# Front of a hybrid layer: ada product by column tiles on TensorE, its loads by row blocks, x turned and projected in two halves

## Chip, core and metric

The kernel runs on one core of a Trainium2 chip. The metric is the device time of one execution in microseconds (us). TensorE is called PE in the profile (its weight loads PEld), VectorE DVE, ScalarE ACT, GpSimd POOL; SyncE (SP) only issues loads and stores. Everything is float32 unless told otherwise.

## What is computed

One layer on 1024 tokens of width 1024: modulated norm, a projection into four parts, a gated recurrence beside a spatial gating unit, an output projection, then a mixture of 32 experts with 4 per token. The change touches the first lines:

```python
c_act = jax.nn.silu(c)
mod = c_act @ ada_w[l] + ada_b[l]                    # [1, 1024] @ [1024, 6144]
sh1, sc1, g1, sh2, sc2, g2 = jnp.split(mod[:, None, :], 6, axis=-1)
z = rmsnorm(h, norm1_g[l]) * (1.0 + sc1) + sh1       # h = x, [1024, 1024]
proj = z @ w_in[l]                                   # [1024, 1024] @ [1024, 2048]
xa, ya, u, v = jnp.split(proj, [D_LRU, 2 * D_LRU, 2 * D_LRU + D_SGU], axis=-1)
```

`sh1` and `sc1` are the first 2048 of the 6144 ada columns; they alone are needed for `z`.

## The kernel before, in words

Five programs, one per engine, run beside one another and are ordered by semaphores. Engines other than SP and POOL work through their programs strictly in the order written.

**Order of loads.** `DENSE` (L55) is the list of 2 MB weight loads, in order: ada 0 to 3, win 0, ada 4, ada 5, win 1, and so on; "ada j" is columns 512 j to 512 j + 511 of `ada_w`, "win j" the same of `w_in`. They rotate through four slots of `big` (`ring`). SP (from L389) first loads 11 small parameter tensors, then runs through `DENSE`: loads 0 to 3 at once; ahead of load 4 (win 0) the eight x tiles of 128 tokens, 512 KB each (L398 to L400); from load 4 on each load waits until its slot is free: `gemv_made` counts finished ada products, `filled` counts PSUM banks that TensorE has filled. A load is laid out (k p) n -> p k n, so each of its rows in memory is 512 columns, 2 KB. POOL (L514) waits for the third `gemv_made` and then issues 13 small transfers (gating weights, gate matrices, biases, two blocks of zeros), 2.75 MB with many rows under 512 B.

**Order of banks.** `bank_jobs` (L69) is the list of everything that passes through the eight PSUM banks, in TensorE's order, with the engine that drains each; a job takes the bank of the job eight places ahead of it once that is drained. `open_bank`, `take` and `drained_before` turn the list into waits.

**Ada product (VectorE).** `mod_products(j)` (L1260) multiplies the eight row blocks of ada j with the eight columns of silu(c), one instruction of 128x512 each, adding up in `gacc[:, j % 2]`: one at L1267, seven at L1269. TensorE's `mod_cols(j)` (L861) sums over the partitions, four matmuls against a column of ones (L867), two instructions each; `mod_add(j)` (L1274) adds the bias. j = 0 to 3 come first; then `scale1` = norm1_g (1 + sc1) (L1290, L1291), which raises `affine_made`.

**x.** ScalarE squares each x tile as it lands (L658, scratch in the memory of `zT`, k = 0), takes the root (L659), for all eight tiles; then it waits for `affine_made` and drains the even k of `zT` (L666), first for tokens 0 to 511 (th = 0), then for the others. VectorE scales the eight tiles by their 1/rms (L1304, L1305) and drains the odd k (`modulate`, L1298). TensorE turns x: for each th and k four transposes of 128x128 into one bank (L898); th = 0 waits for four scaled tiles, th = 1 for eight. When both halves of `zT` are drained and win 0 is there, it projects `xa`: four m by two th, eight matmuls of 128x512 each, two instructions per matmul (`project`, L881).

**Behind it.** VectorE copies each bank of `xa` to `xaT` (L1354), runs `conv(0)` (L1329, L1331) and ada products 4 and 5 in between, then builds the rows of g1 (L1366, L1372). TensorE does `mod_cols(4)`, `mod_cols(5)`, the g1 rows (L875), the turning of the gating weights (L915), and then `ya` with `win 1`. Then follow gates, recurrence, `u`, `v`, output projection, router, and from about 520 us on the expert loop (L1118, L1144: matmuls in column tiles of 32).

Of the kernel before, what the change touches and what calls it, by code (L numbers as in the profile page):

```python
# [20 lines left out]
P = 128  # L21
# [47 lines left out]
def bank_jobs():  # L69

    jobs = [("cols", 0, "dve")]
    jobs += [("mod", j, "dve") for j in range(4)]
    jobs += [("zT", (k, th), "dve" if k % 2 else "act") for th in range(2) for k in range(KT)]
    jobs += [("xa", (m, th), "dve") for m in range(CT) for th in range(2)]
    jobs += [("mod", j, "dve") for j in (4, 5)]
# [57 lines left out]
def build(nc, ins, out):  # L133
# [8 lines left out]
    with ExitStack() as ctx:  # L142
        def sb(name, shape, dt=F32):
            return ctx.enter_context(nc.sbuf_tensor(name, shape, dt))
# [10 lines left out]
        def ring(key):  # L155
            return big[:, DENSE_AT[key] % DENSE_SLOTS, :].rearrange("p (k n) -> p k n", k=8)

        lru_t = big[:, 4, :].rearrange("p (i n) -> p i n", i=4)
        s5 = big[:, 5, :]
# [56 lines left out]
        cols = sb("cols", [P, NROWS])  # L216
        cact = sb("cact", [P, KT])
        mod = sb("mod", [P, 48])
# [171 lines left out]
        def _(sp_):  # L390
# [6 lines left out]
            for n, (kind, j) in enumerate(DENSE):  # L397
                if n == DENSE_SLOTS:  # L398
                    for t in range(TT):
                        sp_.dma_start(x_rows[:, t, :], x[t * P:(t + 1) * P, :]).then_inc(x_in[t], SEMW)  # L400
                if n >= DENSE_SLOTS:
                    old, i = DENSE[n - DENSE_SLOTS]
                    if old == "ada":
                        sp_.wait_ge(gemv_made, i + 1)
                    else:
                        last = ("v", TT - 1) if i == 3 else (("xa", "ya", "u")[i], (CT - 1, 1))
                        sp_.wait_ge(filled, JOB[last] + 1)
                w = {"ada": ada_w, "win": w_in, "wout": w_out}[kind]
                sp_.dma_start(ring((kind, j)), w[:, j * 512:(j + 1) * 512].rearrange("(k p) n -> p k n", p=P)
                              ).then_inc(dense_in[n % DENSE_SLOTS], SEMW)  # L410
# [63 lines left out]
        def _(pool):  # L474
            chain = [0]

            def link(ins_):

                chain[0] += 1
                ins_.then_inc(pool_chain, 1)  # L480
                pool.wait_ge(pool_chain, chain[0])

            link(pool.memset(ident[:, :], 0.0))
            link(pool.affine_select(out=ident[:, :], in_=ident[:, :], compare_op=ALU.not_equal, fill=1.0, base=0,
# [152 lines left out]
        def _(act):  # L637
# [15 lines left out]
            act.wait_ge(dve_drained, 1)  # L653
            act.activation(cact[:, :], cols[:, ROW["c"]:ROW["c"] + 8], ACT.Silu).then_inc(cact_made, 1)

# [194 lines left out]
        def _(pe):  # L850
# [38 lines left out]
            pe.transpose(b[:, 0:NROWS], prow[0:NROWS, :], ident[0:NROWS, 0:NROWS]).then_inc(filled, 1)  # L889
            for j in range(4):  # L890
                mod_cols(j)

            for th in range(2):
                pe.wait_ge(x_scaled, 4 * th + 4)
                for k in range(KT):
# [3 lines left out]
                    last.then_inc(filled, 1)  # L899
            dense_ready(("win", 0))  # L900
            for who, drained in (("act", act_drained), ("dve", dve_drained)):
                pe.wait_ge(drained, drained_before(JOB[("zT", (KT - 1, 1))], who))
            for m in range(CT):
                for th in range(2):
                    project("xa", ("win", 0), m, th)
# [328 lines left out]
        def _(dve):  # L1234
# [24 lines left out]
            def mod_products(j):  # L1259

                n = DENSE_AT[("ada", j)]
                dve.wait_ge(dense_in[n % DENSE_SLOTS], SEMW * (n // DENSE_SLOTS + 1))
                if j >= 2:

                    dve.wait_ge(filled, JOB[("mod", j - 2)] + 1)
# [9 lines left out]
            def mod_add(j):  # L1275
                b = take("mod", j)
                dve.tensor_tensor(mod[:, 4 * j:4 * j + 4], b[:, 0:4], col("ada_b", 4 * j, 4), ALU.add
                                  ).then_inc(dve_drained, 1)

            dve.wait_ge(cact_made, 1)  # L1280
            mod_products(0)
            mod_products(1)
            mod_add(0)
            mod_products(2)
            mod_add(1)
            mod_products(3)
            mod_add(2)
            mod_add(3)
            dve.wait_ge(dve_drained, drained_by(JOB[("mod", 3)])[1])
            link(dve.tensor_scalar(scale1[:, :], mod[:, SC1:SC1 + 8], 1.0, None, ALU.add))  # L1290
# [10 lines left out]

            for t in range(TT):
                dve.wait_ge(sqrt_made, t + 1)
                link(dve.reciprocal(rstd[:, t:t + 1], srt[:, t:t + 1]))  # L1304
                dve.tensor_scalar(x_rows[:, t, :], x_rows[:, t, :], rstd[:, t:t + 1], None, ALU.mult).then_inc(x_scaled, 1)  # L1305
            for th in range(2):
                modulate("zT", th, lambda k: zT[:, k, th * 512:(th + 1) * 512], scale1, SH1)

# [42 lines left out]
            for m in range(CT):  # L1351
                for th in range(2):
                    b = take("xa", (m, th))
                    dve.tensor_copy(xaT[:, m, th * 512:(th + 1) * 512], b).then_inc(dve_drained, 1)  # L1354
                if m == 0:
                    dve.wait_ge(dve_drained, drained_by(JOB[("xa", (0, 1))])[1])
                    conv(0)
                if m < 2:
                    mod_products(4 + m)
# [348 lines left out]
```

## Time and profile before

| what | value |
|---|---|
| median of 3 runs | 2366.47 us (2357.96, 2366.47, 2366.7) |
| profiled execution, its own time | 2362.14 us |
| its span, first to last instruction | 2360.4 us |
| instructions | 53160 |
| TensorE busy | 2133.1 us, 90% |
| VectorE, ScalarE, GpSimd busy | 767.7, 387.2, 436.2 us |
| mean granted TensorE clock | 0.961 |
| DMA | 525.82 MB, mean 223 GB/s |
| gate/up and down matmuls of the expert loop (L1118, L1144) | 1021.9 and 529.3 us busy |

"Idle before, releaser" in a row tells how long the engine stood still ahead of it and what ended that. Rows of SPq and POOLq are issues of transfers, not their duration. A granted clock of 1.00 is 2.4 GHz, 0.50 is 1.2 GHz.

### The profile page before, as it was taken

To read this page: it belongs to the slowest core of one execution; us is meant where nothing else is said; L and a number is where in the kernel's file an instruction comes from. 1 tells how busy PE (TensorE), PEld (TensorE's weight loads), DVE (VectorE), ACT (ScalarE), POOL (GpSimd) and SP (SyncE) were. 2 spreads that over 40 slices of the span, in tenths; PEclk is the share of its full clock that TensorE was granted. 3 is DMA by queue.
4 is the path that set the end of the run, shared out by engine and by line. 5 is a ranking of instruction groups with operands and counts; after the bars stand their busy time and mean duration, and the time that the engine had idled before them with its cause. 6 is when DMAs were issued, how large, how long until landed. Compare 5 with 4: busy or idle time off the path is not lost.

```text
span 2360.4 us, 53160 instructions
## 1 busy us (share of the span) xinstructions
PE 2133.1 (90%) x21037; PEld 921.1 (39%) x21038; DVE 767.7 (33%) x2033; ACT 387.2 (16%) x866; POOL 436.2 (18%) x420
## 2 busy tenths in 40 slices
PE   3998989949999999999898879889999888989995
PEld 3443444423443434334333224334443333443342
DVE  6437744242323222222223223223222232222223
ACT  3035122121111111011111101111111111010112
POOL 2000022021222122222212112212221221221221
PEclk9999999969999999999999899989999999999997
DMA  9312215141653529365499999599988659944345
GB/s 335 114 62 107 107 42 228 69 150 35 222 171 125 215 56 366 96 238 191 149 390 347 403 390 380 206 402 383 398 320 316 223 186 401 371 150 140 95 163 171
DMA packets 142462, 525.82 MB, mean 223 GB/s; under 512 B 14672, under 2 KB 45376, under 8 KB 109664
## 3 DMA queue, kind: packets, MB, share of 16 engines
q1 hardware_dynamic: 111728, 470.39, 51.6%
q0 software_dynamic: 30704, 55.06, 10.0%
q8 instruction: 15, 0.25, 0.0%
q14 instruction: 15, 0.12, 0.0%
HBM read 493.02 MB, written 32.37 MB: 223 GB/s over the span
## 4 chain that ended last, share of the span: by engine, by line
PE 69%; DMA 9%; issue 8%; DVE 7%; ACT 2%; POOL 2%; SPq 2%; DVEq 1%; POOLq 0%; ACTq 0%
PE psum L1118 32%; PE psum L1144 19%; PE psum L1014 4%; PE psum L881 4%; DMA r<-hs_rows,idx_next 3%; DMA big<-in_exp_w_gu_dram 3%; PE psum L976 2%; DMA big<-in_exp_w_down_dram 2%; PE psum L1085 1%; PE psum L1130 1%; PE psum L1072 1%; DMA big<-in_w_in_dram 1%; POOL r L595 1%; DVEq L341 1%; PE psum L923 1%
## 5 line engine op out<-in xcount | busy, mean ns | idle before, releaser
L1118 PE MATMUL psum<-big,r 128*32 128x512 f32 x9152 | 1021.9, 600 | 32.2 <-DMA big<-in_exp_w_gu_dram 31.5
L1118 PEld LDWEIGHTS psum<-big,r 128*32 128x32 f32 x9152 | 285.6, 110 | 684.7 <-issue 624.0
L1144 PE MATMUL psum<-big,r 128*32 128x256 f32 x9152 | 529.3, 385 | 18.2 <-issue 14.0
L1144 PEld LDWEIGHTS psum<-big,r 128*32 128x32 f32 x9152 | 293.6, 111 | 228.8 <-issue 53.6
L588 POOL DMA_INDIRECT acc_rows<-r,sidx_cur x143 | 225.3, 1576 | 497.1 <-DVE r L1640 467.2
L788 ACT ACTIVATE r<-r 128x256 f32<-128x256 f32 x143 | 59.3, 414 | 1266.3 <-DVE r L1627 1266.3
L595 POOL TENSOR_TENSOR r<-r 128x256 f32<-128x256 f32 x143 | 104.3, 730 | 831.6 <-ACT r L788 831.6
L1621 DVE TENSOR_TENSOR r<-psum,r 128x256 f32<-128x256 f32 x143 | 60.7, 425 | 519.1 <-PE psum L1118 519.1
L1637 DVE TENSOR_TENSOR r<-psum,r 128x256 f32<-128x256 f32 x143 | 60.7, 424 | 432.0 <-PE psum L1144 432.0
L881 PE MATMUL psum<-r,big 128*128 128x512 f32 x384 | 167.9, 598 | 1.4 <-DMA big<-in_w_in_dram 1.4
L781 ACT ACTIVATE r<-psum,mod,scale 128x128 f32<-128x128 f32 x384 | 141.9, 460 | 28.0 <-PE psum L1085 28.0
L1085 PE MATMUL psum<-ident,r 128*128 128x128 f32 x384 | 68.4, 307 | 54.9 <-DMA r<-hs_rows,idx_next 54.9
L1632 DVE TENSOR_TENSOR r<-r 128x256 f32<-128x256 f32 x143 | 60.8, 425 | 168.7 <-POOL r L595 168.7
L1014 PE MATMUL psum<-big,r 128*128 128x512 f32 x256 | 111.1, 594 | 0.6 <-DMA big<-in_w_out_dram 0.4
L881 PEld LDWEIGHTS psum<-r,big 128*128 128x128 f32 x384 | 73.2, 192 | 92.9 <-issue 91.3
L793 ACT ACTIVATE r<-psum 128x256 f32<-128x256 f32 x143 | 55.1, 386 | 296.3 <-PE psum L1130 296.3
L1085 PEld LDWEIGHTS psum<-ident,r 128*128 128x128 f32 x384 | 48.9, 156 | 94.9 <-DMA r<-hs_rows,idx_next 62.2
L1014 PEld LDWEIGHTS psum<-big,r 128*128 128x128 f32 x256 | 48.3, 190 | 62.6 <-issue 61.3
L577 POOL DMA_INDIRECT r<-hs_rows,idx_next x48 | 48.1, 1003 | 128.4 <-DVE idx_next L1588 125.8
L1640 DVE SCALAR_TENSOR_TENSOR r<-r,g1row 128x256 f32<-128x256 f32 x143 | 69.4, 485 | 5.1
L1130 PE MATMUL psum<-ident,r 128*128 128x128 f32 x286 | 62.0, 300 | 6.4 <-DVE r L1632 6.4
L1269 DVE SCALAR_TENSOR_TENSOR gacc<-big,cact,gacc 128x512 f32<-128x512 f32 x84 | 63.1, 752 | 3.0
(233 smaller groups left out, 1118.8 us busy)
## 6 DMA issues: line engine op xcount, KB each, us to landing
big<-in_exp_w_gu_dram SPq DMA_DIRECT2D x256, 1024.0 KB, 7.7
big<-in_exp_w_down_dram SPq DMA_DIRECT2D x128, 1024.0 KB, 16.2
big<-in_ada_w_dram SPq DMA_DIRECT2D x12, 2048.0 KB, 12.9
r<-in_x_dram SPq DMA_DIRECT2D x16, 512.0 KB, 12.6
big<-in_w_in_dram SPq DMA_DIRECT2D x4, 2048.0 KB, 19.1
r<-in_exp_b_gu_dram SPq DMA_DIRECT2D x128, 64.0 KB
big<-in_w_out_dram SPq DMA_DIRECT2D x2, 2048.0 KB, 13.3
hs_rows<-r POOLq DMA_DIRECT2D x8, 512.0 KB, 3.2
```

Of the source, the lines that this page charges most:

```text
L588: pool.indirect_dma_start(acc_quarters, bass.IndirectOffsetOnAxis(ap=sidx_cur[:, u:u + 1], axis=0), y_sb[:, u, :], None, bounds_check=4 * ...
L595: pool.tensor_tensor(gsig_sb[:, u % 2, :], gate_sb[:, u % 2, :], sig_sb[:, u % 2, :], ALU.mult).then_inc(gsig_made, 1)
L781: ins_ = act.activation(izT[:, k, :], psum[:, 6 + half, i * P:(i + 1) * P], ACT.Identity, bias=mod[:, SH2 + k:SH2 + k + 1], scale=scale2[: ...
L881: last = pe.matmul(b, w[:, k, m * P:(m + 1) * P], zT[:, k, th * 512:(th + 1) * 512], start=(k == 0), stop=(k == KT - 1))
L1014: last = pe.matmul(b, src[:, ct % CT, t * P:(t + 1) * P], ring(("wout", dh))[:, ct, :], start=(ct == 0), stop=(ct == 2 * CT - 1))
L1085: last = pe.transpose(psum[:, 6 + half, i * P:(i + 1) * P], zg[:, k * P:(k + 1) * P], ident[:, :])
L1118: last = pe.matmul(psum[32 * j:32 * j + 32, u, :].rearrange("p (a n) -> p a n", a=2), izT[:, k, u * UNIT:(u + 1) * UNIT], rhs[:, :, 256 * ...
L1130: last = pe.transpose(psum[:, u, h * P:(h + 1) * P], act_sb[:, u % 2, h * P:(h + 1) * P], ident[:, :])
L1144: ins_ = pe.matmul(psum[32 * i:32 * i + 32, 4 + u % 2, 0:256], actT[:, u, h, 32 * j:32 * j + 32], down_slab(f)[:, 256 * i:256 * i + 256], ...
L1269: ins_ = dve.scalar_tensor_tensor(out=a, in0=w[:, k, :], scalar=cact[:, k:k + 1], in1=a, op0=ALU.mult, op1=ALU.add)
L1632: dve.tensor_tensor(act_sb[:, u % 2, :], lin_u, gsig_sb[:, u % 2, :], ALU.mult).then_inc(act_made, 1)
L1640: dve.scalar_tensor_tensor(out=y_sb[:, u, :], in0=y_sb[:, u, :], scalar=sgate_cur[:, u:u + 1], in1=g2_rows, op0=ALU.mult, op1=ALU.mult).th ...
```

## The change

The first 2048 columns of the ada product go to TensorE. Loads 0 to 3 of `DENSE` become row blocks: load j brings rows 256 j to 256 j + 255, all 2048 columns (rows of 8 KB). silu(c) is written into column 0 of eight 32-column stationary tiles `cact_cols`, whose other columns are zero. For each k, four matmuls write four column tiles (32 partitions each) of one bank, one for each 512 columns; the sum over all k ends there as four rows, at partitions 0, 32, 64 and 96. VectorE copies the bank to `gacc`, and four matmuls against every 32nd column of `ident` put the 2048 sums back on the partitions (job "mods"). x tiles 0 to 3 are issued ahead of win 0, tiles 4 to 7 behind it. TensorE turns and projects tokens 0 to 511, then the others. VectorE's program follows that order. ScalarE's program changes in one line, the destination of silu(c).

```diff
@@ -68,10 +68,10 @@
 
 def bank_jobs():
 
-    jobs = [("cols", 0, "dve")]
-    jobs += [("mod", j, "dve") for j in range(4)]
-    jobs += [("zT", (k, th), "dve" if k % 2 else "act") for th in range(2) for k in range(KT)]
-    jobs += [("xa", (m, th), "dve") for m in range(CT) for th in range(2)]
+    jobs = [("cols", 0, "dve"), ("ada", 0, "dve"), ("mods", 0, "dve")]
+    for th in range(2):
+        jobs += [("zT", (k, th), "dve" if k % 2 else "act") for k in range(KT)]
+        jobs += [("xa", (m, th), "dve") for m in range(CT)]
     jobs += [("mod", j, "dve") for j in (4, 5)]
     jobs += [("g1row", q, "dve") for q in range(2)]
     jobs += [("wm", q, "dve") for q in range(2)]
@@ -155,6 +155,9 @@
         def ring(key):
             return big[:, DENSE_AT[key] % DENSE_SLOTS, :].rearrange("p (k n) -> p k n", k=8)
 
+        def ada_pair(j):
+            return big[:, j, :].rearrange("p (k n) -> p k n", k=2)
         lru_t = big[:, 4, :].rearrange("p (i n) -> p i n", i=4)
         s5 = big[:, 5, :]
         ln_g = s5[:, 0:512]
@@ -214,7 +217,8 @@
         before = lru_t[:, 0, 0:P]
         prow = r2[:, 0:P]
         cols = sb("cols", [P, NROWS])
-        cact = sb("cact", [P, KT])
+        cact_cols = sb("cact_cols", [P, KT, UNIT])
+        cact = cact_cols[:, :, 0]
         mod = sb("mod", [P, 48])
         scale1 = sb("scale1", [P, KT])
         scale2 = sb("scale2", [P, KT])
@@ -395,8 +399,8 @@
                 sp_.dma_start(prow[ROW[name]:ROW[name] + rows, :], src.rearrange(pat, p=P)).then_inc(param_in, SEMW)
 
             for n, (kind, j) in enumerate(DENSE):
-                if n == DENSE_SLOTS:
-                    for t in range(TT):
+                if n in (DENSE_SLOTS, DENSE_SLOTS + 1):
+                    for t in range(4 * (n - DENSE_SLOTS), 4 * (n - DENSE_SLOTS) + 4):
                         sp_.dma_start(x_rows[:, t, :], x[t * P:(t + 1) * P, :]).then_inc(x_in[t], SEMW)
                 if n >= DENSE_SLOTS:
                     old, i = DENSE[n - DENSE_SLOTS]
@@ -405,6 +409,11 @@
                     else:
                         last = ("v", TT - 1) if i == 3 else (("xa", "ya", "u")[i], (CT - 1, 1))
                         sp_.wait_ge(filled, JOB[last] + 1)
+                if n < DENSE_SLOTS:
+                    sp_.dma_start(ada_pair(j), ada_w[2 * P * j:2 * P * (j + 1), 0:2048].rearrange("(k p) n -> p k n", p=P)
+                                  ).then_inc(dense_in[n], SEMW)
+                    continue
                 w = {"ada": ada_w, "win": w_in, "wout": w_out}[kind]
                 sp_.dma_start(ring((kind, j)), w[:, j * 512:(j + 1) * 512].rearrange("(k p) n -> p k n", p=P)
                               ).then_inc(dense_in[n % DENSE_SLOTS], SEMW)
@@ -480,6 +489,7 @@
                 ins_.then_inc(pool_chain, 1)
                 pool.wait_ge(pool_chain, chain[0])
 
+            link(pool.memset(cact_cols[:, :, :], 0.0))
             link(pool.memset(ident[:, :], 0.0))
             link(pool.affine_select(out=ident[:, :], in_=ident[:, :], compare_op=ALU.not_equal, fill=1.0, base=0,
                                     pattern=[[-1, P]], channel_multiplier=1))
@@ -651,7 +661,7 @@
 
             act.wait_ge(const_made, 1)
             act.wait_ge(dve_drained, 1)
-            act.activation(cact[:, :], cols[:, ROW["c"]:ROW["c"] + 8], ACT.Silu).then_inc(cact_made, 1)
+            act.activation(cact, cols[:, ROW["c"]:ROW["c"] + 8], ACT.Silu).then_inc(cact_made, 1)
 
             for t in range(TT):
                 act.wait_ge(x_in[t], SEMW)
@@ -887,8 +897,24 @@
             pe.wait_ge(const_made, 1)
             b = open_bank("cols", 0)
             pe.transpose(b[:, 0:NROWS], prow[0:NROWS, :], ident[0:NROWS, 0:NROWS]).then_inc(filled, 1)
-            for j in range(4):
-                mod_cols(j)
+            b = open_bank("ada", 0)
+            pe.wait_ge(cact_made, 1)
+            for n in range(4):
+                dense_ready(("ada", n))
+                for kk in range(2):
+                    k = 2 * n + kk
+                    for i in range(4):
+                        last = pe.matmul(b[32 * i:32 * i + 32, :], cact_cols[:, k, :], ada_pair(n)[:, kk, 512 * i:512 * i + 512],
+                                         start=(k == 0), stop=(k == KT - 1), skip_group_check=True)
+                last.then_inc(gemv_made if n < 3 else filled, 1)
+            b = open_bank("mods", 0)
+            wait_drained(pe, JOB[("ada", 0)])
+            for i in range(4):
+                last = pe.matmul(b[:, 4 * i:4 * i + 4], gacc[:, 0, i * P:(i + 1) * P], ident[:, 0:P:UNIT],
+                                 start=(i == 0), stop=True, skip_group_check=True)
+                if i == 0:
+                    last.then_inc(gemv_made, 1)
+            last.then_inc(filled, 1)
 
             for th in range(2):
                 pe.wait_ge(x_scaled, 4 * th + 4)
@@ -897,11 +923,10 @@
                     for i in range(4):
                         last = pe.transpose(b[:, i * P:(i + 1) * P], x_rows[:, 4 * th + i, k * P:(k + 1) * P], ident[:, :])
                     last.then_inc(filled, 1)
-            dense_ready(("win", 0))
-            for who, drained in (("act", act_drained), ("dve", dve_drained)):
-                pe.wait_ge(drained, drained_before(JOB[("zT", (KT - 1, 1))], who))
-            for m in range(CT):
-                for th in range(2):
+                dense_ready(("win", 0))
+                for who, drained in (("act", act_drained), ("dve", dve_drained)):
+                    pe.wait_ge(drained, drained_before(JOB[("zT", (KT - 1, th))], who))
+                for m in range(CT):
                     project("xa", ("win", 0), m, th)
             for j in (4, 5):
                 mod_cols(j)
@@ -1260,7 +1285,7 @@
 
                 n = DENSE_AT[("ada", j)]
                 dve.wait_ge(dense_in[n % DENSE_SLOTS], SEMW * (n // DENSE_SLOTS + 1))
-                if j >= 2:
+                if j >= 6:
 
                     dve.wait_ge(filled, JOB[("mod", j - 2)] + 1)
                 w, a = ring(("ada", j)), gacc[:, j % 2, :]
@@ -1277,16 +1302,20 @@
                 dve.tensor_tensor(mod[:, 4 * j:4 * j + 4], b[:, 0:4], col("ada_b", 4 * j, 4), ALU.add
                                   ).then_inc(dve_drained, 1)
 
+            def scale_x(t):
+                dve.wait_ge(sqrt_made, t + 1)
+                link(dve.reciprocal(rstd[:, t:t + 1], srt[:, t:t + 1]))
+                dve.tensor_scalar(x_rows[:, t, :], x_rows[:, t, :], rstd[:, t:t + 1], None, ALU.mult).then_inc(x_scaled, 1)
             dve.wait_ge(cact_made, 1)
-            mod_products(0)
-            mod_products(1)
-            mod_add(0)
-            mod_products(2)
-            mod_add(1)
-            mod_products(3)
-            mod_add(2)
-            mod_add(3)
-            dve.wait_ge(dve_drained, drained_by(JOB[("mod", 3)])[1])
+            b = take("ada", 0)
+            dve.tensor_copy(gacc[:, 0, :], b).then_inc(dve_drained, 1)
+            scale_x(0)
+            b = take("mods", 0)
+            dve.tensor_tensor(mod[:, 0:16].rearrange("p (i b) -> p b i", b=4), b[:, 0:16].rearrange("p (b i) -> p b i", b=4),
+                              col("ada_b", 0, 16).rearrange("p (i b) -> p b i", b=4), ALU.add).then_inc(dve_drained, 1)
+            dve.wait_ge(dve_drained, drained_by(JOB[("mods", 0)])[1])
             link(dve.tensor_scalar(scale1[:, :], mod[:, SC1:SC1 + 8], 1.0, None, ALU.add))
             dve.tensor_tensor(scale1[:, :], scale1[:, :], col("norm1_g", 0, 8), ALU.mult).then_inc(affine_made, 1)
             dve.wait_ge(affine_made, 1)
@@ -1299,12 +1328,15 @@
                                       ).then_inc(dve_drained, 1)
 
 
-            for t in range(TT):
-                dve.wait_ge(sqrt_made, t + 1)
-                link(dve.reciprocal(rstd[:, t:t + 1], srt[:, t:t + 1]))
-                dve.tensor_scalar(x_rows[:, t, :], x_rows[:, t, :], rstd[:, t:t + 1], None, ALU.mult).then_inc(x_scaled, 1)
-            for th in range(2):
-                modulate("zT", th, lambda k: zT[:, k, th * 512:(th + 1) * 512], scale1, SH1)
+            for t in range(1, 4):
+                scale_x(t)
+            modulate("zT", 0, lambda k: zT[:, k, 0:512], scale1, SH1)
+            for t in range(4, TT):
+                scale_x(t)
+            for m in range(CT):
+                b = take("xa", (m, 0))
+                dve.tensor_copy(xaT[:, m, 0:512], b).then_inc(dve_drained, 1)
+            modulate("zT", 1, lambda k: zT[:, k, 512:1024], scale1, SH1)
 
             dve.wait_ge(sp_exp, 2)
             link(dve.tensor_scalar(sp[:, 3, :], sp[:, 2, :], 2.0, None, ALU.add))
@@ -1349,9 +1381,8 @@
                 dve.wait_ge(lru_made, ct + 1)
 
             for m in range(CT):
-                for th in range(2):
-                    b = take("xa", (m, th))
-                    dve.tensor_copy(xaT[:, m, th * 512:(th + 1) * 512], b).then_inc(dve_drained, 1)
+                b = take("xa", (m, 1))
+                dve.tensor_copy(xaT[:, m, 512:1024], b).then_inc(dve_drained, 1)
                 if m == 0:
                     dve.wait_ge(dve_drained, drained_by(JOB[("xa", (0, 1))])[1])
                     conv(0)
```

## Rows read from the trace of the kernel before

**Rows 1.** the page: span, and busy time with share of each engine

```profile
span 2360.4 us, 53160 instructions
...
PE 2133.1 (90%) x21037; PEld 921.1 (39%) x21038; DVE 767.7 (33%) x2033; ACT 387.2 (16%) x866; POOL 436.2 (18%) x420
```

**Rows 2.** chain of waits, 20 to 125 us (start, us, what)

```profile
25.50 28.87 DMA big<-in_w_in_dram
...
54.41 55.20 PE psum L881 x128
...
117.44 7.73 PE psum L881 x18
```

**Rows 3.** timeline of SP's queue, 0 to 60 us (start, us, what)

```profile
4.84 9.95 SPq L409 DMA_DIRECT2D big<-in_ada_w_dram  x4
14.83 10.63 SPq L400 DMA_DIRECT2D r<-in_x_dram  x8
25.50 0.98 SPq L409 DMA_DIRECT2D big<-in_w_in_dram  x1
```

**Rows 4.** windows: busy us by engine, clock, DMA share, GB/s

```profile
20.00:28.00 8.00, 2.64 (x12) 2.47 (x12) 7.64 (x13) 0.00 (x0) 0.00 (x0) 1.00 1.05 387
28.00:36.00 8.00, 1.86 (x8) 1.78 (x8) 7.64 (x13) 5.59 (x11) 4.93 (x8) 1.00 1.04 409
36.00:44.00 8.00, 2.67 (x12) 2.59 (x13) 5.83 (x16) 5.25 (x12) 4.05 (x6) 1.00 1.03 281
1240.00:1250.00 10.00, 10.00 (x92) 3.23 (x88) 3.91 (x13) 3.30 (x9) 2.19 (x3) 1.00 1.01 421
```

**Rows 5.** timeline of ScalarE, 28 to 60 us

```profile
30.31 1.06 ACT L658 ACTIVATE r<-r 128x1024 f32<-128x1024 f32 x1 [20.93 <-DMA r<-in_x_dram]
...
44.47 1.06 ACT L658 ACTIVATE r<-r 128x1024 f32<-128x1024 f32 x1 [2.06 <-DMA r<-in_x_dram]
...
45.85 1.43 ACT L666 ACTIVATE r<-psum,mod,scale 128x512 f32<-128x512 f32 x2
```

**Rows 6.** timeline of POOL, 0 to 60 us

```profile
31.07 1.15 POOL L515 DMA_DIRECT2D r<-in_sgu_w_dram  x1 [24.14 <-DVE gacc L1269]
```

**Rows 7.** timeline of all engines: turning and draining x

```profile
43.20 9.81 PE L898 MATMUL psum<-ident,r 128*128 128x128 f32 x64 [4.56 <-DVE r L1305]
...
48.62 5.24 DVE L1298 TENSOR_SCALAR r<-psum,scale,mod 128x512 f32<-128x512 f32 x6 [0.25 <-PE psum L898]
```

**Rows 8.** timelines: column tiles, single 32-column matmuls, mod reduction

```profile
546.56 3.64 PE L1118 MATMUL psum<-big,r 128*32 128x512 f32 x32
...
478.78 7.03 PE L1001 MATMUL psum<-r,big 128*32 128x512 f32 x16 [0.20 <-ACT r L764]
...
24.82 1.87 PE L867 MATMUL psum<-ones,gacc 128*128 128x1 f32 x8 [4.04 <-DVE gacc L1269]
```

**Rows 9.** windows: transposes (L898) alone twice, then all of TensorE

```profile
43.00:48.00 5.00, 4.80 (x23) 4.81 (x24) 1.00 1.03 340
49.00:53.00 4.00, 4.00 (x37) 3.77 (x35) 1.00 1.04 408
...
114.00:116.00 2.00, 2.00 (x4) 0.81 (x4) 0.69 (x1) 0.00 (x0) 0.00 (x0) 0.50 1.05 407
```

**Rows 10.** expert loop: windows with the clock, first and second gate stage

```profile
523.60:526.00 2.40, 2.33 (x12) 0.68 (x16) 0.92 (x6) 0.00 (x0) 0.39 (x1) 0.50 0.00 0
...
523.67 22.15 PE L1118 MATMUL psum<-big,r 128*32 128x512 f32 x192 [0.49 <-issue]
...
571.44 20.74 PE psum L1118 x192
```

**Rows 11.** timeline of VectorE, 60 to 118 us

```profile
68.45 0.69 DVE L1354 COPY r<-psum 128x512 f32<-128x512 f32 x1 [6.17 <-PE psum L881]
...
73.87 0.48 DVE L1267 TENSOR_SCALAR gacc<-big,cact 128x512 f32<-128x512 f32 x1
74.38 5.48 DVE L1269 SCALAR_TENSOR_TENSOR gacc<-big,cact,gacc 128x512 f32<-128x512 f32 x7
```

## Prediction

> **What bounds the kernel now.** I read the page first: TensorE is busy for 90% of the span [rows 1], and the costly groups lie in the expert loop, which the change does not touch. So the change can only move the moment at which the rest starts. I then read the chain of waits for the first 125 us [rows 2]. SP issues loads; the load of `win 0` ends that stretch, 28.87 us after its issue; TensorE runs the `xa` projection from 54.41 to 109.61; small steps follow, and `ya` starts at 117.44. Two paths meet at 54.4: the bytes of `win 0`, and x scaled, turned and modulated. The second ends with VectorE's last drain at 48.62 + 5.24 = 53.86 [rows 7], only 0.5 us earlier. After `xa`, every load is released by work on TensorE or VectorE (`filled`, `gemv_made`), so nothing behind `xa` is tied to the start of the program: **the change is worth what it moves the end of `xa`**, with no cushion and no discount.
>
> The DMA queue is the second thing to see. SP issues ada 0 to 3, eight x tiles and `win 0` [rows 3], and its queue lands them in that order. The engines are full all the time, at 387 GB/s on the 2 KB rows of ada, 409 with the 4 KB rows of x, 281 while POOL's small transfers mix in [rows 4]. ScalarE gets the first x tile at 30.31 and the last at 44.47, and only after squaring the last one does it start on the `zT` drains, at 45.85 [rows 5].
>
> **Bytes.** Moved are four ada blocks (8.39 MB), four x tiles (2.10), `win 0` (2.10), then the other four x tiles (2.10). Up to the last x tile these are the same 14.7 MB that ended with `win 0` before, and POOL's transfers lie in front of it both times: released by the third `gemv_made`, they went out from 31.07 on [rows 6]; now the third block releases them at about 25, and they still end before 53. The issue of `win 0` now waits for block 0's product (about 15 us), with 10 MB already queued: nothing. Ada rows become 8 KB wide. The nearest row for that width is a stretch of expert weights at 421 GB/s; 8.39 MB take 21.7 us at 387 and 19.9 at 421, between 0 and 1.8 saved, I take 1.5. So the last x tile lands at 54.4 - 1.5 = **52.9** (before: 44.5), and `win 0` some 5 us ahead of it. The Trainium skill (DMA: Bandwidth & Descriptors, section Bandwidth) says that loads from HBM are bound near 358 GB/s per core; by that wider rows would save nothing and everything would come 1.5 us later. The trace does not agree: it is at 387 to 421.
>
> **The ada product.** Removed: four passes of eight VectorE instructions, about 6 us each (0.48 + 5.48 us, [rows 11]), and their 16 small matmuls. Each of the four small reductions on TensorE takes 1.87 us [rows 8]. Added: 32 matmuls of 32 columns by 512, two instructions each, in four column tiles. The expert loop shows such groups: 32 instructions in 3.64 us, against 16 in 7.03 for single 32-column matmuls one after another [rows 8]. So a block of 16 instructions costs 1.8 us, twice that at the lower clock; blocks land 5 us apart, and the last, at about 27, is worked off by 31. The copy (0.7), four matmuls against ident (at most 1.9), the addition (0.2) and scale1 (0.6) give scale1 at about 35. Nothing waits for it before 52.9: free, with 18 us of cover. POOL's added memset (0.3 us) hides behind the first ada landing.
>
> **x, first half.** Tile 3 lands in the middle of POOL's transfers, near 39; squared and scaled by 42; 32 transposes. These ran 23 in 5 us early and 37 in 4 us later [rows 9], so the first half takes up to 6.9 us and is turned by 49. VectorE drains the odd k. **ScalarE does not drain the even k**: its program is not in the diff. It squares all eight tiles, then drains. It sits on tile 4 to 7 with the zT drains queued behind, TensorE waits for those drains ahead of `xa`, and the first half's early start is lost. From tile 7: square to first drain 45.85 - 44.47 = 1.38 us, four drains about 2.75 (two take 1.43, [rows 5]), 0.1 to wake: `xa` starts at **57.1** instead of 54.41, **+2.7**.
>
> **Clock.** TensorE then has been idle since about 49. After such a pause, at the start of the expert loop, the granted clock is 0.50 (the 1.2 GHz level) up to 526, and 192 instructions take 22.15 us against 20.74 [rows 10]. Bounds 0 and 1.6; I take **+1.4**. Before, the pause was 1.4 us.
>
> **The turn between the halves.** Before, all 64 transposes stood ahead of `xa`. Now 32 stand between its halves, exposed: 32 at 37 in 4 us are 3.5 us, the last VectorE drain 0.85 behind (53.86 against 53.01), 0.1 to wake. That is **+4.4**. Bounds: 3.0, if drains follow closer, and 7.5 at the earlier rate of the transposes. The halves themselves are the same 128 instructions, 55.2 us.
>
> **VectorE in the second half.** conv(0) and two ada products must now fit into 27.6 us instead of 55. Copy, convolution and product 4 took 68.45 to 79.86 [rows 11], 11.4 us; a copy and product 5 add 6.7, and a copy 0.7. From the first full bank (6.9) that is 25.7: 1.9 us of cover, gone if anything there gets longer, and then TensorE's `mod 5` step would wait. I cost it at nothing. The scale_x of tiles 4 to 7 and the `zT` drains of half 1 are on VectorE ahead of this and inside the terms above.
>
> **Sum.** 2.7 + 1.4 + 4.4 = +8.5 us: `xa` ends at 118.1 instead of 109.6. The profiled execution took 2362.14 us (span 2360.4), so it would be 2370.6. It lies 4.3 below the median of the three runs, 2366.47; against that median: **2375.0**. That is 0.36% slower, and about 0.5% (11.8 us) is what a measurement can tell from no change: the runs alone lie 8.7 us apart. So I call it "same", on the slow side.
>
> **Rivals.**
> *A, the halves do overlap with the loads as drawn (faster).* If tiles 4 to 7 were there before ScalarE needs them, `xa` would start when half 0 is turned, at 49 (`win 0` lands at 47 to 48): 49.2 + 27.6 + 4.4 + 27.6 = 108.8, 0.8 us less than before, 2365.7. For it: the ada path is free early. Against: 17.4 MB would have to land by 45, at 458 GB/s over 38 us, and no row shows more than 421. Even then the gain stays inside 0.5%. Chance 5%.
> *B, the clock falls in the turn (slower).* If transposes do not keep TensorE at the 2.4 GHz level, the second half's 32 take the early rate, 0.22 us each (7.0 instead of 3.5), and its projection starts at 1.2 GHz (+1.4): +13.4 in all, 2379.9. It decides when 4.4 us without a plain matmul let the clock fall. For it: between 109.6 and 113.7 small matmuls did not hold it (0.50 from 114 to 116, [rows 9]), and the rate of the early transposes was the lower one. Against: in that same run of transposes the rate rose to 37 in 4 us with nothing but transposes running [rows 9]. The Trainium skill (TensorE: Matmul & The Clock Gate, Part 4) says that transposes do not count as busy for the clock in the same way, which would give this case; the row speaks against it. Chance 14%.
> *C, the column tiles do not overlap.* Then a block costs 6.9 us at full clock and 13.8 at half; the product would end between 41 and 68, and the halves are turned only behind it: in the second case `xa` starts near 79 instead of 57.1, 2397. [rows 8] speak against it. Chance 2%.
> *Forecast*: 79%.
>
> **How the numbers follow.** The forecast's own terms run from 2.4 + 0 + 3.0 = +5 (ada rows at the full 421, no cold start, drains close behind) to 4.2 + 1.6 + 4.4 = +10 (no gain from wider rows; a longer turn is case B), and the scatter of medians adds some 3 us to either side. The range, **2365 to 2382**, takes in A and B and leaves out C and the far scatter. Slower by over 0.5%: half or more of B, all of C, an eighth of the forecast, 0.19. Faster by over 0.5%: scatter alone, 0.03. Within: 0.78.
>
> **What would show it.** Right: ScalarE's square of the last x tile at about 53 and the first `zT` drain over 1 us later; TensorE idle from about 49 to 57 although `win 0` has landed; `xa` in two stretches of 27 to 29 us with 4.4 us between them; its end near 118; the rest shifted unchanged. Wrong: the last x tile before 48, ScalarE draining `zT` before it, a clock of 0.50 behind the turn (B), scale1 later than 50 (C), a wait of TensorE at `mod 5`, or `ya` starting less late than `xa` ends.

## The result, and the profile after

The changed kernel takes 2372.52 us (median of 10 runs, 2367.96 to 2381.77) against 2365.23 of the kernel before (10 runs); the ratio is 1.0041, with a 95% interval of 1.0025 to 1.0057. By the ratio that is +9.7 us, by the plain difference of the two medians +7.3; forecast were +8.5. The time lies inside the range of 2365 to 2382, and the change is inside 0.5%, on the slow side. The profiled execution took 2371.42 us, its span is 2369.7, 9.3 more than before.

ScalarE first. Timeline of the changed kernel from 28 us on; line numbers have moved (L668 squares x, L676 drains `zT`, L924 turns x, L891 projects, L907 is the ada product):

```profile
28.78 1.06 ACT L668 ACTIVATE r<-r 128x1024 f32<-128x1024 f32 x1 [19.02 <-DMA r<-in_x_dram]
...
34.57 1.06 ACT L668 ACTIVATE r<-r 128x1024 f32<-128x1024 f32 x1 [0.30 <-DMA r<-in_x_dram]
...
49.43 1.06 ACT L668 ACTIVATE r<-r 128x1024 f32<-128x1024 f32 x1 [13.38 <-DMA r<-in_x_dram]
...
53.54 1.04 ACT L668 ACTIVATE r<-r 128x1024 f32<-128x1024 f32 x1
...
54.91 2.77 ACT L676 ACTIVATE r<-psum,mod,scale 128x512 f32<-128x512 f32 x4
```

The first x tile is there at 28.78, where [rows 5] had 30.31: the 8 KB rows saved 1.5 us over the four ada blocks, as taken. Tile 3 is squared at 34.57. Then ScalarE stands still for 13.38 us until tile 4 lands at 49.43, squares four tiles without a pause, and drains the first even k of half 0 only at 54.91. TensorE meanwhile (timeline of PE):

```profile
27.51 1.93 PE L907 MATMUL psum<-big,cact_cols 128*32 128x512 f32 x16 [1.62 <-DMA big<-in_ada_w_dram]
...
37.08 5.10 PE L924 MATMUL psum<-ident,r 128*128 128x128 f32 x32 [5.70 <-DVE r L1309]
57.77 30.73 PE L891 MATMUL psum<-r,big 128*128 128x512 f32 x64 [15.59 <-ACT r L676]
88.34 3.66 PE L924 MATMUL psum<-ident,r 128*128 128x128 f32 x32
93.10 27.70 PE L891 MATMUL psum<-r,big 128*128 128x512 f32 x64 [1.11 <-DVE r L1327]
```

The last ada block takes 1.93 us, half 0 is turned by 42.2, and 15.59 us pass until ScalarE's drain lets the first half of `xa` start at 57.77. The profile puts the wait down to ScalarE (ACT), not to a load. The first half takes 30.73 us, the second 27.70; between them 32 transposes and 1.11 us of waiting for VectorE's drain. `xa` ends at 120.80; it was 109.61 [rows 2]. The chain of waits runs through the same points:

```profile
16.75 32.66 DMA r<-in_x_dram
...
57.77 30.73 PE psum L891 x64
88.50 3.51 PE psum L924 x32
92.03 0.82 DVE r L1327
```

And the granted clock in the first microseconds of `xa` (windows: PE, PEld, DVE, ACT, POOL busy, clock, DMA share, GB/s):

```profile
57.70:60.00 2.30, 2.23 (x3) 1.17 (x4) 0.00 (x0) 0.00 (x0) 0.00 (x0) 0.50 1.05 387
...
62.00:64.00 2.00, 2.00 (x4) 0.80 (x3) 0.00 (x0) 0.00 (x0) 0.00 (x0) 0.53 1.05 387
64.00:66.00 2.00, 2.00 (x6) 0.83 (x5) 0.00 (x0) 0.00 (x0) 0.00 (x0) 1.00 1.05 386
88.00:90.00 2.00, 2.00 (x18) 1.72 (x17) 1.28 (x2) 0.93 (x2) 0.00 (x0) 1.00 0.00 0
```

The clock is at 0.50, the 1.2 GHz level, until about 63.9, 6 us into the projection. At the turn, from 88 on, it is 1.00.

### The profile page after: what moved, and what is told of

It reads as the page before. It is cut to its first block, busy times and chain, and to the rows that moved or that the text cites. A ratio compares the mean times of both kernels' runs of the same rounds, so it can differ in the third digit from the quotient of the medians.

```text
span 2369.7 us, 53206 instructions
## 1 busy us (share of the span) xinstructions
PE 2134.4 (90%) x21077; PEld 916.0 (39%) x21078; DVE 746.7 (32%) x1999; ACT 386.7 (16%) x866; POOL 436.9 (18%) x421
## 4 chain that ended last, share of the span: by engine, by line
PE 69%; DMA 10%; issue 8%; DVE 6%; ACT 3%; POOL 2%; SPq 2%; DVEq 1%; POOLq 0%; ACTq 0%
PE psum L1143 32%; PE psum L1169 18%; PE psum L1039 4%; PE psum L891 4%; DMA big<-in_exp_w_gu_dram 4%; DMA r<-hs_rows,idx_next 2%; PE psum L1001 2%; PE psum L1155 1%; PE psum L1110 1%; DMA r<-in_x_dram 1%; PE psum L1097 1%; POOL r L605 1%; SPq L457 1%; DVEq L345 1%; DMA big<-in_exp_w_down_dram 1%
## 5 line engine op out<-in xcount | busy, mean ns | idle before, releaser
L891 PE MATMUL psum<-r,big 128*128 128x512 f32 x384 | 170.2, 603 | 16.7 <-ACT r L676 15.6
L891 PEld LDWEIGHTS psum<-r,big 128*128 128x128 f32 x384 | 74.2, 194 | 109.5 <-issue 109.5
L1599 DVE TENSOR_TENSOR r<-r 128x1024 bf16 x49 | 60.1, 1226 | 3.6
```

The lines of the kernel that those rows point to most:

```text
L891: last = pe.matmul(b, w[:, k, m * P:(m + 1) * P], zT[:, k, th * 512:(th + 1) * 512], start=(k == 0), stop=(k == KT - 1))
```

## The experiments

Each is judged by two numbers: where `xa` ends in its profile, which is one execution, and the ratio of its time to the kernel before, run beside it, which rests on 6 to 12 executions. The table gathers them, with the start and end of `xa` in us; the last column is the ratio's excess over 1, times 2363 us, about the median of the kernel before in these comparisons. An interval of 0.0012 to either side is 3 us. The delay of e5 is told in its own section.

| kernel | xa starts | xa ends | against before | ratio (95%) | time against before |
|---|---|---|---|---|---|
| before | 54.41 | 109.61 | | | |
| changed | 57.77 | 120.80 | +11.2 | 1.0041 (1.0025 to 1.0057) | +9.7 |
| e1_scalar_halves | 48.20 | 110.53 | +0.9 | 1.0011 (1.0000 to 1.0021) | +2.6 |
| e2_ada_only | 55.73 | 110.90 | +1.3 | 1.0008 (0.9996 to 1.0020) | +1.9 |
| e6_pool_late_only | 48.31 | 110.13 | +0.5 | 1.0009 (0.9997 to 1.0021) | +2.1 |
| e3_pool_late | 44.10 | 104.11 | -5.5 | 0.9977 (0.9967 to 0.9987) | -5.4 |
| e4_kept_busy | 57.34 | 117.36 | +7.8 | 1.0028 (1.0018 to 1.0039) | +6.6 |
| e7_tilewise_turn | 41.57 | 103.04 | -6.6 | 0.9967 (0.9955 to 0.9979) | -7.8 |
| e8_turn_hidden | 40.40 | 99.07 | -10.5 | 0.9957 (0.9944 to 0.9970) | -10.2 |
| e9_ada_only_pool_late | 48.16 | 103.33 | -6.3 | 0.9962 (0.9948 to 0.9975) | -9.0 |
| e10_before_pool_late | 53.99 | 109.16 | -0.4 | 0.9997 (0.9978 to 1.0015) | -0.7 |

### Is it ScalarE's order?

```diff
-            for t in range(TT):
-                act.wait_ge(x_in[t], SEMW)
-                link(act.activation(r1[:, 0:D], x_rows[:, t, :], ACT.Square, accum_out=ssum[:, t:t + 1]))
+            for th in range(2):
+                for t in range(4 * th, 4 * th + 4):
+                    act.wait_ge(x_in[t], SEMW)
+                    link(act.activation(r2[:, 5120:6144], x_rows[:, t, :], ACT.Square, accum_out=ssum[:, t:t + 1]))
...
+                if th == 0:
+                    act.wait_ge(affine_made, 1)
                 for k in range(0, KT, 2):
```

> The changed kernel with ScalarE's program in halves as well: it squares x tiles 0 to 3, drains the even k of half 0, then squares tiles 4 to 7 and drains half 1 (the squares' scratch moves to unused memory). Theory (ScalarE's order held half 0 back behind the x tiles 4 to 7): the first zT drain near 38, xa starts when win 0 has landed, at 48 to 49 instead of 57.8, and ends near 110 instead of 120.8; the program comes within 0.15% of the kernel before, some 10 us under the changed one. Rival (the late start comes from the loads, not from the order of ScalarE): xa still starts at 56 to 58 and the time stays that of the changed kernel.

Timelines of ScalarE and of PE:

```profile
37.84 0.78 ACT L676 ACTIVATE r<-psum,mod,scale 128x512 f32<-128x512 f32 x1 [2.25 <-PE psum L924]
...
42.85 0.78 ACT L676 ACTIVATE r<-psum,mod,scale 128x512 f32<-128x512 f32 x1 [0.87 <-PE psum L924]
49.46 1.06 ACT L669 ACTIVATE r<-r 128x1024 f32<-128x1024 f32 x1 [5.84 <-DMA r<-in_x_dram]
```

```profile
48.20 30.03 PE L891 MATMUL psum<-r,big 128*128 128x512 f32 x64 [4.96 <-DMA big<-in_w_in_dram]
...
82.83 27.70 PE L891 MATMUL psum<-r,big 128*128 128x512 f32 x64 [1.11 <-DVE r L1327]
```

ScalarE drains half 0 from 37.84 on and waits for tile 4 afterwards, when nobody is waiting for it. `xa` starts at 48.20, released by `win 0`, 9.6 us earlier than in the change, and ends 10.3 earlier. The theory holds: with the same loads, and tile 4 there at 49.46 as in the change, the order alone takes nearly the whole loss away. The rival, that the loads alone made the start late, is out. The loads have a part in it all the same, since the old order costs this much only because tile 4 lands so late; e6 below takes away the other half of the pair. The repaired change is still no faster than the kernel before: what it wins at the start (6.2 us) it gives to the turn between the halves (4.6 us from the end of one half to the start of the other) and to a first half at the lower clock (30.03 where the second takes 27.70).

### Does the ada product on TensorE cost anything?

```diff
+    jobs += [("zT", (k, th), "dve" if k % 2 else "act") for th in range(2) for k in range(KT)]
+    jobs += [("xa", (m, th), "dve") for m in range(CT) for th in range(2)]
...
-                if n in (DENSE_SLOTS, DENSE_SLOTS + 1):
-                    for t in range(4 * (n - DENSE_SLOTS), 4 * (n - DENSE_SLOTS) + 4):
+                if n == DENSE_SLOTS:
+                    for t in range(TT):
```

TensorE and VectorE go back to the order of before (both halves turned, then `xa`); the rest of the change stays.

> The ada product on TensorE with its row-block loads kept, the halves undone: all x tiles ahead of win 0, both halves turned ahead of xa, VectorE's order as before. Theory (the ada part is free and all of the loss is in the halves): win 0 lands 1 to 2 us earlier than before thanks to the wider rows, xa starts at 53 to 54.4 and ends near 109, time within 3 us of the kernel before. Rival (the ada product on TensorE costs by itself, by its waits or by a colder clock): xa ends at 112 or later.

```profile
45.71 1.06 ACT L667 ACTIVATE r<-r 128x1024 f32<-128x1024 f32 x1 [1.07 <-DMA r<-in_x_dram]
```

```profile
37.54 6.61 PE L923 MATMUL psum<-ident,r 128*128 128x128 f32 x32 [6.11 <-DVE r L1309]
48.23 6.39 PE L923 MATMUL psum<-ident,r 128*128 128x128 f32 x32 [4.08 <-DVE r L1309]
55.73 55.17 PE L890 MATMUL psum<-r,big 128*128 128x512 f32 x128 [1.11 <-DVE r L1327]
```

The time came out as expected, within 3 us of the kernel before. The profile did not: `xa` starts at 55.73, 1.3 us later than before and 1.3 beyond the expected span, and ends at 110.90, between the two expectations. The last x tile is squared at 45.71 (before: 44.47), although the queue had gained 1.5 us by tile 0; and half 1 is turned in 6.39 us with the clock at 0.50 to nearly 54, behind a pause of 4.08 us. The first of these pointed at POOL: its transfers are released by the third ada block, 5 us earlier than before (26.23 in the changed kernel against 31.07, [rows 6]), and so push in among the x tiles.

### POOL's transfers moved out of the way

```diff
-            pool.wait_ge(gemv_made, 3)
+            pool.wait_ge(filled, JOB[("xa", (0, 0))] + 1)
```

The same line was put into four kernels: the repaired change (e3), the change as it is (e6), the ada part alone (e9) and the kernel before (e10).

> The kernel of e1_scalar_halves, and POOL's 13 small transfers wait for the first filled bank of xa instead of the third ada block. Theory (what then bounds the start of xa is the queue in front of win 0, a third of it POOL's): win 0 lands near 38.5, half 0 is turned and drained by 42, xa starts at 42 and ends at 102 to 103; 7 to 8 us under the kernel before, about 2358, ratio 0.997. Rival (what is gained in front is taken back, because the postponed transfers hold up ya or the loads of ada 4 and 5): ya starts no earlier than in e1_scalar_halves.

> The changed kernel with POOL's transfers postponed alone, ScalarE's order as in the change. Theory: x tile 4 lands near 40.5 instead of 49.4, four squares (5.5 us) and four drains (2.8) later xa starts, at 49, and ends near 111; ScalarE's order still costs what e3_pool_late is faster by, 7 to 9 us. Rival (ScalarE's order is no cost of its own once the tiles are early): xa ends within 2 us of e3_pool_late.

> The kernel of e2_ada_only with POOL's transfers postponed to the first filled bank of xa. In e2_ada_only the last x tile was worked on at 45.71 and xa started at 55.73, later than before. Theory (POOL's transfers, released 5 us earlier by the third ada block, and half 1 turned at the lower clock after a pause of 4 us): the last x tile is there by 41, half 1 is turned by 50 and xa starts at 50 to 51, ends near 106. Rival (the ada product on TensorE itself makes the late start): xa starts at 54 or later.

> The kernel before with POOL's transfers postponed alone. Theory (two paths met at 54.4, win 0's bytes and VectorE's ada products with the scaling, turning and draining of x behind them, 0.5 us apart): win 0 lands near 45, but VectorE still finishes its last drain near 53.9, so xa starts near 54 and the time is that of the kernel before within 1 us; the ada product must leave VectorE for anything to be won in front. Rival (the queue of loads alone was the bound): xa starts at 50 or earlier.

PE timelines of e3 and e6, and ScalarE's of e6:

```profile
36.64 6.35 PE L924 MATMUL psum<-ident,r 128*128 128x128 f32 x32 [3.67 <-DVE r L1309]
44.10 27.70 PE L891 MATMUL psum<-r,big 128*128 128x512 f32 x64 [1.11 <-DVE r L1327]
```

```profile
48.31 29.52 PE L891 MATMUL psum<-r,big 128*128 128x512 f32 x64 [5.47 <-ACT r L676]
...
82.43 27.70 PE L891 MATMUL psum<-r,big 128*128 128x512 f32 x64 [1.11 <-DVE r L1327]
```

```profile
39.27 1.06 ACT L668 ACTIVATE r<-r 128x1024 f32<-128x1024 f32 x1 [3.69 <-DMA r<-in_x_dram]
...
45.44 2.77 ACT L676 ACTIVATE r<-psum,mod,scale 128x512 f32<-128x512 f32 x4
```

In e6 tile 4 is squared at 39.27 instead of 49.43: 2.75 MB of POOL's transfers had cost the queue 10.2 us there. `xa` starts at 48.31, still held back by ScalarE, which drains from 45.44 on, and ends 10.7 us earlier than in the change. So the loss of the change has two conditions, ScalarE's old order and the x tiles 4 to 7 landing behind POOL's transfers, and taking away either one (e1 by 10.3 us, e6 by 10.7) gives nearly all of it back.

With both (e3) `xa` starts at 44.10. Between e3 and e6 its end differs by 6.0 us, which is what ScalarE's order costs once the tiles are early: 4.2 at the start and 1.8 by the clock, as the first half takes 29.52 us in e6 behind a longer pause and 27.70 in e3. 7 to 9 were expected. e3 missed its 42 by 2 us: `win 0` is there, and TensorE turns half 0 until 43.0, in 6.35 us, most of it at the lower clock, behind the fourth scaled tile. The postponed transfers do not hold up `ya`: it starts at 111.71 in e3, 118.36 in e1.

PE timelines of e9 and of e10:

```profile
37.37 8.84 PE L923 MATMUL psum<-ident,r 128*128 128x128 f32 x64 [3.39 <-DVE r L1309]
48.16 55.17 PE L890 MATMUL psum<-r,big 128*128 128x512 f32 x128 [1.96 <-DVE r L1327]
```

```profile
43.02 9.86 PE L898 MATMUL psum<-ident,r 128*128 128x128 f32 x64 [4.23 <-DVE r L1305]
53.99 55.17 PE L881 MATMUL psum<-r,big 128*128 128x512 f32 x128 [1.11 <-DVE r L1298]
```

In the kernel before, the late transfers alone gain nothing: the wait ahead of `xa` changes its name, from the load of `win 0` to VectorE's drain (idle before L881: 1.11 <-DVE), and its end by 0.4 us. The ada product on TensorE alone gains nothing either (e2). Together (e9) they gain 9.0 us of time (some 3 to either side) and 6.3 at the end of `xa`, and this without any halves. The late start of e2 was thus not the ada product's; e9 starts at 48.16, 2 us earlier than expected, since its 64 transposes ran without a pause (8.84 us).

### The first half's 3 us

```diff
+                if th == 0:
+                    wait_drained(pe, JOB[("zT", (1, 0))])
+                    for _ in range(14):
+                        pe.matmul(bank_of(JOB[("zT", (1, 0))]), x_rows[:, 0, 0:P], x_rows[:, 0, 0:512],
+                                  start=True, stop=True)
```

> The changed kernel with 14 added matmuls of 128x512 on x rows (results unused, into a bank that is already drained), which TensorE does while it waits for ScalarE, between the turning of half 0 and xa. Theory (the 3 us by which the first half of xa took longer, 30.73 against 27.70, are the lower clock after the pause): the first half takes 27.7, xa starts at the same time, 57.8, and ends near 117.8; the time falls by 3 us to about 0.28% above the kernel before. Rival (the first half is slow for another reason, such as the loads of ada 4, ada 5 and win 1 that run beside it): 30.7 again.

```profile
43.24 12.18 PE L929 MATMUL psum<-r 128*128 128x512 f32 x28
57.34 27.70 PE L891 MATMUL psum<-r,big 128*128 128x512 f32 x64 [1.92 <-ACT r L676]
...
89.65 27.71 PE L891 MATMUL psum<-r,big 128*128 128x512 f32 x64 [1.11 <-DVE r L1332]
```

```profile
58.00:60.00 2.00, 2.00 (x7) 0.80 (x6) 0.00 (x0) 0.00 (x0) 0.00 (x0) 1.00 1.06 389
```

The first half takes 27.70 us like the second, beside the same loads (389 GB/s in that window, 387 in the change). The clock, at 1.00 here and at 0.50 for 6.1 us in the change, is the 3.0 us: 6.1 us at half the rate are worth 3. By its end `xa` gains 3.4 us, 0.4 of them an earlier start; the ratio goes from 1.0041 to 1.0028, which is 3.1 us, though the two intervals overlap. (The profiled execution of e4 itself has a span of 2375.9 us: single executions scatter by more than this, which is why the end of `xa` is read from profiles and the time from the ratio.)

### Does a microsecond in front count in full?

```diff
+            wait_drained(pe, JOB[("xa", (0, 1))])
+            for _ in range(48):
+                pe.matmul(bank_of(JOB[("xa", (0, 1))]), xaT[:, 0, 512:512 + P], xaT[:, 0, 512:1024],
+                          start=True, stop=True)
             for j in (4, 5):
```

> The changed kernel with 48 added matmuls of 128x512 (unused) between the end of xa and the small steps behind it: a delay of 41.4 us at that point. Theory (nothing behind xa is tied to the start of the program): the program takes 41 us longer than the changed kernel, about 2414. Rival (loads or work of other engines behind xa have slack of their own and absorb a part): 35 us or less.

```profile
120.26 41.20 PE psum L933 x96
...
169.30 27.47 PE psum L891 x64
```

The median of 4 runs is 2413.43 us, 40.9 above the changed kernel's, for 41.2 us of added matmuls; the ratio, 1.0214 against 1.0041, says the same, and the two intervals leave some 6 us to either side. So nothing behind `xa` is seen to absorb them. The table says the same for small shifts: its two columns of differences agree within 3 us throughout.

### A version that beats both

e7 is e3 with half 0 turned as its tiles come, e8 moves the turn of half 1 ahead of the last quarter of half 0:

```diff
+            for i in range(4):
+                pe.wait_ge(x_scaled, i + 1)
+                for k in range(KT):
...
             half_drained(0)
-            for m in range(CT):
+            for m in range(CT - 1):
                 project("xa", ("win", 0), m, 0)
+            pe.wait_ge(x_scaled, TT)
...
+            project("xa", ("win", 0), CT - 1, 0)
+            half_drained(1)
```

> The kernel of e3_pool_late, half 0 turned tile by tile as the four x tiles are scaled, not after the fourth. Theory (what bounds the start of xa there is the turning behind the fourth tile, 6.35 us of transposes at the lower clock): the last eight transposes end near 38.5, the drains near 41, xa starts at 41 and ends at 101.5, 2 to 3 us under e3_pool_late; about 2355.5, ratio 0.9965. Rival (win 0 lands no earlier than 43): xa starts at 44 again.

> The kernel of e7_tilewise_turn, half 1 turned ahead of the last quarter of half 0's projection, so that its drains run beside that quarter. Theory (of the 4.6 to 4.7 us between the halves the transposes are 3.5 and the tail of the drains 1.1): the tail goes, TensorE runs without a pause from the start of xa to its end, which comes 1.1 us earlier, near 100.5; about 2354.5. Rival: VectorE, which now copies the last quarter behind the drains, makes it wait and nothing is won.

```profile
41.57 29.18 PE L891 MATMUL psum<-r,big 128*128 128x512 f32 x64 [2.61 <-DVE r L1336]
...
75.34 27.70 PE L891 MATMUL psum<-r,big 128*128 128x512 f32 x64 [1.11 <-DVE r L1336]
```

```profile
40.40 20.84 PE L892 MATMUL psum<-r,big 128*128 128x512 f32 x48 [2.61 <-DVE r L1342]
61.07 3.66 PE L940 MATMUL psum<-ident,r 128*128 128x128 f32 x32
64.57 34.50 PE L892 MATMUL psum<-r,big 128*128 128x512 f32 x80
98.90 1.84 PE L878 MATMUL psum<-ones,gacc 128*128 128x1 f32 x16
```

e7 starts `xa` at 41.57 instead of 44.10, yet ends it only 1.1 us before e3, because its first half loses 1.5 us to the clock again (29.18). e8 has no row with idle time between 40.40 and 98.90, and ends at 99.07, 10.5 us before the kernel before and 4.0 before e7. Of these 4.0 only 1.1 or so, the tail of the drains that is now hidden, come from its edit, as expected. 1.2 come from an earlier start and some 1.5 from the clock in the first half: its first 48 instructions take 20.84 us, as at full clock. Up to the first three quarters of half 0 TensorE's program is the same in both kernels, so these 2.7 are a difference between two executions: both have a pause of 2.61 us ahead of `xa`, and behind it the clock is at 0.50 in e7 (42 to 44 us) and at 1.00 in e8. The profiled execution of e8 was also the fastest of its six, 2344.62 us with a median of 2351.53. Its ratio of 0.9957 is the lowest of all, but its interval overlaps with those of e7 and of e9, which does without halves. That e8 beats e7 or e9 is not shown; that all three beat both the changed kernel and the kernel before is.

## Why the prediction was right

**The start of `xa`**: forecast 57.1, measured 57.77. ScalarE's order holds it back, as said, and e1 shows it. One step of the working was off though: the forecast hung on the landing of the last x tile (52.9) plus 1.38. In the profile the path is the landing of tile 4 (49.4), four squares at 1.37 without a pause, then the drains; the last square starts at 53.54, 0.6 us later than the forecast had it. The lateness of tile 4, with POOL's transfers ahead of it, was in the sum, but as a given and not as a cause; e6 shows that it is the other condition of the loss.

**POOL's share.** Tile 3 was expected at 39 and squared at 34.57; half 0 was turned by 42.2, not 49. POOL's transfers, issued from 26.23, had hardly begun to take their share, and took it from `win 0` and tiles 4 to 7. That varies: in e5, whose program is the same up to the end of `xa`, tile 3 is squared at 36.94, and `xa` starts at 57.77 all the same. It made no difference, since ScalarE held everything anyway. The 8 KB rows run at 424 GB/s from 18 to 23 us; 421 was the most that the forecast's terms allowed them.

**The clock** was the term that was mis-sized: +1.4 taken, bounds 0 and 1.6, measured 30.73 - 27.70 = **3.0**. The price came from one row, the start of the expert loop [rows 10], where the low level lasts under 3 us of plain matmuls (0.50 up to 526, 0.89 from 526 to 528). Here it lasted 6.1. One row gave no range.

**The turn**: 4.4 taken, 4.6 measured (88.50 to 93.10: transposes 3.51, VectorE's last drain, 1.11 of waiting in all).

**Sum**: +8.5 forecast, +11.2 at the end of `xa`, which lies outside the +5 to +10 that the forecast's own terms allowed. The difference is 1.6 in the clock term, 0.7 at the start and 0.2 in the turn. The program came out at +9.7 all the same. Three points of the chain of the changed kernel, and one of the kernel before:

```profile
128.93 27.47 PE psum L891 x64
...
264.04 14.40 PE psum L891 x32
...
280.12 27.57 PE psum L1001 x64
```

```profile
253.64 15.36 PE psum L881 x32
```

Between the first and the last lie 151.2 us; before, from 117.44 to 270.68, 153.2. In the other profiles it is 151.1 (e2), 151.9 (e8), 152.5 to 153.2 (e1, e3 to e7), 148.7 (e9) and 149.4 (e10). So 2 us, and up to 4.5, come or go in that stretch, and the forecast's closeness to the time was in part luck: an error of 2.7 us in the front met 2 us the other way behind it. Part of it can be named: the same 32 matmuls near its end take 15.36 us before, 14.40 in the change and 13.73 in e9 and e10, and the granted clock over their first 3.4 us is 0.53, 0.82 and, in e10, 1.00. Whether it differs by kernel or only by execution no run tells; e10 and the kernel before, which differ only in when POOL's transfers go out, are 3.8 us apart here with times that agree.

**Rivals.** A, the overlap as drawn, did not occur. e1, where half 0 starts once `win 0` is there, comes nearest to its size: `xa` ends 0.9 us after the kernel before, not 0.8 ahead of it, as the lower clock costs 2.3 there. B, the clock falling in the turn, is out: it is 1.00 at 88 to 90, and the transposes take 3.66 us in every kernel with halves. C is out: the 16 instructions of the last ada block take 1.93 us, those of the slowest, the first, 3.58, not 6.9 or 13.8. VectorE's cover in the second half was 1.9 us by the working and about 2 in the profile: its third copy of the second half ended at 118.75, TensorE's last bank came at 120.8.

## What to carry to other kernels

When a stage is split into halves to overlap it with loads, look at the program of every engine that touches it: here one engine's program kept the old order, and all that the others had gained waited behind it. Look for all paths that meet at the point which is to move earlier; here there were three (VectorE's ada products, the queue with POOL's transfers in it, ScalarE's order), and in the kernel before, removing one of the first two alone gave nothing (e2, e10), and both together 9 us (e9). A loss can have two conditions in the same way: the change lost by the order and the late tiles together, and mending either one was enough (e1, e6), so one mended cause does not show that it was the only one. And a wait on an engine's count, such as POOL's for the third ada block, moves when that engine gets faster, and what it releases can then get in the way.

## What the runs showed of the hardware that was not expected

**How long the lower clock lasts after a pause differs.** With matmuls back to back, the first half of `xa` took 30.73, 30.16, 30.03, 29.52, 29.18 us in the change, e5, e1, e6 and e7, against 27.70 with TensorE kept busy (e4) and behind a pause of 1.11 us (e3): 1.5 to 3.0 us lost. The length of the pause ahead of it does not settle it: a pause of 15.59 us in the change cost 3.0, one of 13.27 in e5 2.5, one of 5.47 in e6 1.8, one of 4.96 in e1 2.3; one of 2.61 cost 1.5 in e7 and nothing in e8.

**Transposes alone bring the clock back, but not always.** In e9, 64 of them without a pause took 8.84 us, with the clock at 0.50 until 40 and at 1.00 from 42 on; in e2, 32 took 6.39 behind a pause of 4.08 us, with the clock at 0.50 to nearly 54. Two windows, one of each kernel:

```profile
44.00:48.00 4.00, 2.20 (x21) 1.96 (x18) 3.90 (x6) 3.97 (x6) 0.00 (x0) 1.00 1.05 387
```

```profile
50.00:52.00 2.00, 2.00 (x11) 2.00 (x11) 1.82 (x4) 1.30 (x2) 0.00 (x0) 0.50 1.06 389
```

TensorE does nothing but transposes in both, and the ones in the first window end at 46.2. The Trainium skill (TensorE: Matmul & The Clock Gate, Part 4) says that the full clock does not engage for transposes; e9 shows that it can.

**POOL's transfers cost the queue more than their bytes.** 2.75 MB of them moved tile 4 from 39.27 to 49.43: 10.2 us, that is 270 GB/s, where the 4 KB rows run at 409 [rows 4] and the 8 KB rows at 424 (18 to 23 us of the changed kernel). Whether it is their small rows, the two blocks of zeros (1 MB of the 2.75) or the second queue beside SP's, no run separates.
